# Gates stored in DRAM by groups of eight key blocks, and a ring of gated activations four deep

## The chip, the cores and the metric

The kernel runs on one core of one Trainium2 chip. The metric is the device time of one execution in microseconds, as the median over executions. The engines are named PE (TensorE), ACT (ScalarE), DVE (VectorE), POOL (GpSimd) and SP (SyncE). Everything is computed in float32 or in pairs of the reduced float32 type (a "high" and a "low" part).

## What is computed

One layer of a hybrid decoder, for 512 prompt tokens and 8 x 4 sample tokens that share the weights (D_MODEL 1024):

- h <- LN1(ALPHA h + W_out [dilated attention ; SSD scan]), with one combined input projection.
- h <- LN2(ALPHA h + PEER(h)), the part that matters here.

PEER is a retrieval of single-neuron experts. There are 128 x 128 = 16,384 experts. Each of 8 heads scores two halves of a query against 128 sub-keys, and of the sums the 16 best experts are taken, with softmax gates. So each token has 128 experts:

```
act = gelu(einsum('nd,nhkd->nhk', t, u_tab[e]))
out = einsum('nhk,nhkd->nd', g * act, v_tab[e])
```

## The kernel before

**Two ways through the experts.** The first three tiles of 128 prompt tokens (DT = 3, DEN = 384 tokens) are computed densely. For each of the PK = 128 key blocks (128 experts each) the kernel multiplies all 384 tokens with all experts of the block, applies gelu, multiplies with a dense gate table (zero where the expert wasn't chosen), and multiplies with the block's rows of peer_v. The fourth prompt tile and the sample tokens go the sparse way: POOL gathers their rows by an indirect transfer (4 KB a token, 512 KB a gather), first of peer_rows, then of peer_v, into a ring of RING = 8 buffers, and DVE takes dot products (L2022) and weighted sums (L2027) of them. Gathers go through queue q0, the direct transfers of SP through queue q1.

**The up stage** (`sp_up`, `act_up`, `pe_up`, `dve_onehots`). SP fetches a row of peer_u (L1863, 512 KB) into one of four raw buffers; ACT casts the high part (L1571), POOL or, for the later rows, DVE makes the low part (L1578, L2048); PE makes 24 matmuls of a row (`half_up`), three for each of 8 chunks (`product`, L188 to L190); ACT applies gelu into a ring (L1926), and SP stores the result to the DRAM table `act` (L1868, 192 KB). `act` lies by groups of GRP = 4 key blocks, and a group is read back in 6 KB a partition.

**The gate table** is made beside rows 68 to 115 of the up stage. There are SLABS = 12 slabs of SLAB = 32 tokens. DVE makes one-hot tables, PE multiplies them (L2014), ACT copies the result to `slab[n % 2]` (128 partitions x 128 key blocks x 32 tokens, 16 KB a partition, L1962). When a slab is complete, SP stores it (`keep_slab`, L1886) and goes on with the fetches of peer_u rows and the stores of `act`, all in q1. `keep_slab(n - 1)` stands at the start of slab n; that of the last slab stands ahead of the rows from TAIL = 116 on. SP is in order: at row 119 it waits for the last slab store and issues the first gate load, and then fetches rows 124 to 127. DVE is in order too: in the last rows it makes a low part and takes two dot products for each row.

**The value stage** (`sp_values`, `act_values`, `pe_values`, `dve_values`). For key block a, with group a // 4:

- SP loads a group's `act` (L2095, 768 KB) into one of two buffers, when DVE has finished the group before the last; the group's gates (L2099, 768 KB) right behind it, into one of two; and then four rows of peer_v (L2090, 512 KB each) into four raw buffers, each when its buffer is free.
- ACT casts the high part of the row (L2131) into a ring of eight, when PE has finished block a-8, and then the high part of the gated activations (L2135) into a ring of eight, when DVE has made the product.
- DVE multiplies activations with gates (L2208), makes the low part of the row (L2212), takes one or two late rows of the sparse way, and makes the low part of the gated activations (L2216).
- PE makes 18 matmuls (3 token tiles x 2 halves x 3 products), each 512 columns wide, all accumulated in six banks over the 128 blocks.

The semaphores start ahead (`vp_done` at 8, `ga_lo` at 2, `v_lo` at 4, `weighted` at 8), so a wait for `vp_done` of a + 1 asks for block a-8. The final layer norms follow, the first two of them inside the last blocks.

**Where the gates lie.** The DRAM table `gate` is (12 slabs, 128 partitions, 128 key blocks, 32 tokens). A slab store writes 16 KB in one run a partition. The load of a group reads, for each partition, 12 runs (one a slab) of 4 key blocks x 32 tokens, 512 B. On-chip memory is laid out by hand: `cut(at, ...)` and `overlay(at, ...)` place a buffer at `at` KB of each partition. The two rings of gated activations lie at 50 and 62, 12 KB each, the two gate buffers at 26 and 32, 6 KB each.

Of the kernel before, what the change touches and what calls it, by code (L numbers as in the profile page):

```python
# [148 lines left out]
def layer(nc, t):  # L149

    ctx = ExitStack()
    with ctx:
# [25 lines left out]
        def cut(at, *dims):  # L178
            n = int(np.prod(dims))
            assert at * KW + n <= 206 * KW, (at, dims)  # L180
            return shaped(arena[:, int(at * KW):int(at * KW) + n], dims)
# [1673 lines left out]
        def sp_up(sp):  # L1855
# [28 lines left out]
            def keep_slab(n):  # L1884
                sp.wait_ge(g_kept, n * GS + (GS + 4))
                sp.dma_start(t["gate"][n], slab[n % 2]).then_inc(slab_stored[n % 2], 16)  # L1886

# [182 lines left out]

        ga = overlay(50, 8, DEN, kind=F32R), overlay(62, 8, DEN, kind=F32R)
        agrp = [cut(at, GRP, DEN) for at in (132, 142)]
        ggrp = [cut(at, GRP * DEN) for at in (26, 32)]
        vraw, vs = overlay(10, 4, D), (overlay(152, 8, D, kind=F32R), overlay(75, 8, D, kind=F32R))
# [21 lines left out]

        def sp_gates(sp, x, par):
            g = x * 2 + par
            sp.dma_start(ggrp[par].rearrange("p (s a n) -> p s (a n)", a=GRP, n=SLAB),  # L2099
                         t["gate"].rearrange("s p a n -> p s (a n)")[:, :, bass.ds(g * (GRP * SLAB), GRP * SLAB)])\  # L2100
                .then_inc(gate_in[par], 16)

        def sp_values(sp):
            for s in range(2):
                sp.wait_ge(slab_stored[s], 16 * (1 + SLABS // 2))
            for s in range(4):
                sp.wait_ge(a_stored[s], 16 * (GROUPS + 1))
            sp.wait_ge(u_done, PK)

            def group(x, par):  # L2110
                sp_gelus(sp, x, par)
                sp_gates(sp, x, par)
                for k in range(GRP):
                    sp_rows(sp, x, par, k)

            group(0, 1)
            with sp.Fori(1, PAIRS) as x:
                for par in range(2):
                    group(x, par)
            sp.wait_ge(copied, 16 * 48)  # L2120

        def act_values(act):
# [3 lines left out]
            def pair(x, last=False):  # L2126
                for j in range(8):
# [4 lines left out]
                    if last and j == 6:  # L2132
                        act_root(act, TILES, LAST[0])
                    act.wait_ge(weighted, x * 8 + (j + 9))
                    act.copy(ga[0][:, j], prod[j % 2]).then_inc(ga_hi, 1)  # L2135

# [10 lines left out]
        def pe_values(pe):  # L2147
# [4 lines left out]
            def pair(x, first=False, last=False):  # L2152
                for j in range(8):
                    pe.wait_ge(ga_lo, x * 8 + (j + 3))
                    pe.wait_ge(v_lo, x * 8 + (j + 5))
                    for i in range(DT):
                        for half in range(2):
                            mm = product(pe, bank[:, 2 * i + half, :], [w[:, j, i * P:(i + 1) * P] for w in ga],
                                         [v[:, j, half * 512:(half + 1) * 512] for v in vs], first and j == 0, last and j == 7)
# [9 lines left out]
        def dve_values(dve):  # L2169
# [31 lines left out]
            for a in range(PK):  # L2201
                par, k, j = a // GRP % 2, a % GRP, a % 8
                rows_here = range(min(a, ROWS_END) * LATE_ROWS // ROWS_END, min(a + 1, ROWS_END) * LATE_ROWS // ROWS_END)
                if k == 0:
                    dve.wait_ge(a_in[par], 16 * (a // 8 + 1))
                    dve.wait_ge(gate_in[par], 16 * (a // 8 + 1))
                dve.wait_ge(ga_lo, a + 1)
                dve.tensor_tensor(prod[j % 2].rearrange("p (s n) -> p s n", n=SLAB),  # L2208
                                  agrp[par][:, k].rearrange("p (s n) -> p s n", n=SLAB),
                                  ggrp[par].rearrange("p (s a n) -> p s a n", a=GRP, n=SLAB)[:, :, k], ALU.mult).then_inc(weighted, 1)  # L2210
                dve.wait_ge(v_hi, a + 1)
# [3 lines left out]
                dve.wait_ge(ga_hi, a + 1)  # L2215
                dve.tensor_tensor(ga[1][:, j], prod[j % 2], ga[0][:, j].bitcast(F32), ALU.subtract).then_inc(ga_lo, 1)  # L2216
                for r in rows_here[1:]:
# [188 lines left out]
```

## Time and profile before

| | us |
|---|---|
| median of 3 runs | 2153.55 |
| lowest, highest | 2152.06, 2166.17 |
| profiled execution, its own time | 2161.72 |
| its span in the profile | 2159.3 |
| PE busy in the span | 2044.9 (95%) |
| DVE busy | 1485.2 (69%) |
| transfers, mean rate | 316 GB/s |

The profile page shows one execution. Its span begins with the first instruction and ends with the last; the rest of its own time lies around it. The up stage ends at 1592.9 us of the span, the value stage's matmuls run from 1604.8 to about 2136, and the last layer norms end the span. In the rows below, "L188" is a line of the kernel, "overlay" and "arena" are buffers in on-chip memory, "bank" is the matmul accumulator. "Share of 16 engines" is the time of the transfer records over 16 times the stretch; where records overlap it goes over 100%. "Under 2 KB" counts the records smaller than that.

### The profile page before, as it was taken

The numbers are of one execution on the slowest core, as the hardware profiler recorded it, in microseconds if no ns is written. First come the engines' busy times: TensorE is split into PE (matmuls) and PEld (weight loads), VectorE is DVE, ScalarE is ACT, GpSimd is POOL, SyncE is SP. The second block draws the span as 40 slices with busy tenths as digits, with TensorE's granted clock in tenths as the row PEclk, the third lists the DMA queues.
The fourth block names the chain that finished last, engine by engine and source line by source line (L and its number), as shares of the span: only waits on it lengthen the run. The fifth ranks groups of instructions, "written<-read, shape, count | busy, mean of one in ns | idle before, by whom it ended". The sixth has DMA issues, their size and how long they took to land.

```text
span 2159.3 us, 33707 instructions
## 1 busy us (share of the span) xinstructions
PE 2044.9 (95%) x12186; PEld 1709.8 (79%) x12186; DVE 1485.2 (69%) x3108; ACT 742.2 (34%) x1111; POOL 787.3 (36%) x485
## 2 busy tenths in 40 slices
PE   7999999998978997999999999999979999999996
PEld 7999985555542346989999999999978888778784
DVE  1375125664662333678888879999789888988888
ACT  2232113443440001224333355555433333333332
POOL 4343210000210003336898841221365564656440
PEclk9999998999988998999999999999999999999998
DMA  9999987883968668936999977888999999999992
GB/s 325 346 315 311 318 324 292 341 354 139 339 235 318 235 221 323 347 116 223 352 361 357 340 284 274 306 299 302 359 388 390 389 393 393 389 385 391 387 387 104
DMA packets 202346, 682.97 MB, mean 316 GB/s; under 512 B 18305, under 2 KB 84225, under 8 KB 194177
## 3 DMA queue, kind: packets, MB, share of 16 engines
q1 hardware_dynamic: 150832, 439.29, 56.4%
q0 software_dynamic: 46080, 167.79, 20.3%
q10 hardware_dynamic: 5328, 74.52, 9.9%
q8 instruction: 62, 1.02, 0.2%
q14 instruction: 44, 0.35, 0.0%
HBM read 618.78 MB, written 196.32 MB: 377 GB/s over the span
## 4 chain that ended last, share of the span: by engine, by line
PE 58%; DMA 19%; DVE 9%; issue 9%; POOL 3%; ACT 2%; SPq 0%; POOLq 0%; DVEq 0%; ACTq 0%
DMA overlay<-peer_v 15%; PE bank L188 12%; PE bank L189 12%; PE bank L190 12%; PE bank L1426 5%; PE bank L2014 4%; POOL overlay L358 3%; DVE overlay L2212 3%; DVE arena L2027 2%; PE bank L644 2%; PE bank L628 2%; DMA arena<-cache_v 1%; ACT overlay L2131 1%; PE bank L694 1%; PE bank L667 1%
## 5 line engine op out<-in xcount | busy, mean ns | idle before, releaser
L188 PE MATMUL bank<-overlay 128*128 128x384 f32 (+4 forms) x2832 | 959.7, 339 | 46.5 <-DVE overlay L2216 17.0
L189 PE MATMUL bank<-overlay 128*128 128x384 f32 (+4 forms) x2832 | 946.2, 334 | 0.0
L190 PE MATMUL bank<-overlay 128*128 128x384 f32 (+4 forms) x2832 | 945.2, 334 | 0.0
L188 PEld LDWEIGHTS bank<-overlay 128*128 128x128 f32 (+1 forms) x2832 | 535.4, 189 | 87.0 <-issue 39.1
L189 PEld LDWEIGHTS bank<-overlay 128*128 128x128 f32 (+1 forms) x2832 | 535.3, 189 | 30.3
L190 PEld LDWEIGHTS bank<-overlay 128*128 128x128 f32 (+1 forms) x2832 | 534.5, 189 | 31.2
L1850 POOL DMA_INDIRECT arena<-peer_v,arena x160 | 267.4, 1671 | 228.0 <-DVE arena L2027 205.1
L1578 POOL TENSOR_TENSOR overlay<-overlay 128x1024 fp32r<-128x1024 f32 x86 | 206.5, 2404 | 316.0 <-ACT overlay L1571 312.9
L2027 DVE SCALAR_TENSOR_TENSOR arena<-arena 128x1024 f32<-128x1024 f32 x160 | 204.3, 1277 | 0.1
L1850 POOL DMA_INDIRECT arena<-peer_rows,arena x80 | 106.6, 1332 | 245.8 <-DVE arena L2022 225.0
L1571 ACT CAST overlay<-overlay 128x1024 fp32r<-128x1024 f32 x144 | 150.0, 1044 | 114.7 <-DMA overlay<-peer_u 90.6
L2212 DVE TENSOR_TENSOR overlay<-overlay 128x1024 fp32r<-128x1024 f32 x128 | 155.8, 1217 | 45.2 <-ACT overlay L2131 45.2
L2131 ACT CAST overlay<-overlay 128x1024 fp32r<-128x1024 f32 x128 | 134.5, 1051 | 136.6 <-DMA overlay<-peer_v 133.8
L358 POOL TENSOR_TENSOR overlay<-overlay 128x1024 fp32r<-128x1024 f32 x44 | 105.9, 2418 | 178.6 <-ACT overlay L320 178.6
L1926 ACT ACTIVATE arena<-bank 128x384 f32<-128x384 f32 x128 | 63.7, 498 | 209.6 <-PE bank L190 204.1
L2135 ACT CAST overlay<-overlay 128x384 fp32r<-128x384 f32 x128 | 65.7, 513 | 197.6 <-DVE overlay L2208 197.6
L1426 PE MATMUL bank<-arena 128*128 128x512 f32 x256 | 120.1, 622 | 0.0
L1711 DVE SCALAR_TENSOR_TENSOR arena<-arena,bank 128x1024 f32<-128x1024 f32 x80 | 96.4, 1214 | 27.9 <-DMA arena<-peer_rows,arena 27.7
L1962 ACT COPY arena<-bank 128x512 f32<-128x512 f32 x96 | 103.6, 1131 | 33.1 <-PE bank L2014 33.0
L2058 DVE TENSOR_SCALAR arena<-arena 128x128 f32<-128x128 f32 x384 | 106.4, 349 | 0.0
L1426 PEld LDWEIGHTS bank<-arena 128*128 128x128 f32 x256 | 49.0, 198 | 66.1 <-issue 64.6
L2014 PE MATMUL bank<-arena 128*128 128x128 f32 x768 | 101.0, 274 | 0.0
(235 smaller groups left out, 2160.9 us busy)
## 6 DMA issues: line engine op xcount, KB each, us to landing
overlay<-peer_u SPq DMA_DIRECT2D x128, 512.0 KB, 7.6
overlay<-peer_v SPq DMA_DIRECT2D x128, 512.0 KB, 11.3
o_ks<-cache_k ACTq DMA_DIRECT2D x11, 4088.0 KB, 18.4
o_vsall<-cache_vall SPq DMA_DIRECT2D x21, 2044.0 KB, 23.5
arena<-cache_kT SPq DMA_DIRECT2D x32, 896.0 KB, 11.2
arena<-cache_v SPq DMA_DIRECT2D x56, 512.0 KB, 6.9
arena<-w_out SPq DMA_DIRECT2D x48, 512.0 KB, 5.6
act<-arena SPq DMA_DIRECT2D x128, 192.0 KB, 8.2
```

Of the source, the lines that this page charges most:

```text
L188: pe.matmul(out, lhs[0], rhs[0], start=start, stop=False)
L189: pe.matmul(out, lhs[0], rhs[1], start=False, stop=False)
L190: return pe.matmul(out, lhs[1], rhs[0], start=False, stop=stop)
L358: pool.tensor_tensor(ws[1][:, s], wraw[:, s], ws[0][:, s].bitcast(F32), ALU.subtract).then_inc(w_lo, 1)
L1426: mm = pe.matmul(bank[:, 2 * (i % 2) + half, :], mixT[:, c, i * P:(i + 1) * P], w[:, half * 512:(half + 1) * 512], start=(c == 0), stop=(c ...
L1571: act.copy(us[0][:, s], uraw[s]).then_inc(u_hi, 1)
L1578: pool.tensor_tensor(us[1][:, s], uraw[s], us[0][:, s].bitcast(F32), ALU.subtract).then_inc(u_lo, 1)
L1850: pool.indirect_dma_start(gring[g % RING], None, table, bass.IndirectOffsetOnAxis(ap=at, axis=0)).then_inc(row_in[g % RING], 16)
L2014: mm = pe.matmul(bank[:, 4 + w % 4, j * P:(j + 1) * P], hot_b[:, w % 2, j], hot_a[:, w % 2, j], start=True, stop=True)
L2027: dve.scalar_tensor_tensor(acc, gring[r], w[:, bass.ds(j, 1)], acc, ALU.mult, ALU.add).then_inc(row_done, 1)
L2131: act.copy(vs[0][:, j], vraw[:, k]).then_inc(v_hi, 1)
L2212: dve.tensor_tensor(vs[1][:, j], vraw[:, k], vs[0][:, j].bitcast(F32), ALU.subtract).then_inc(v_lo, 1)
```

## The change

The gate table becomes (16 pairs of groups, 128 partitions, 12 slabs, 8 x 32). A slab store writes, for each partition, 16 runs of 1 KB, one for each pair. A gate load now covers a pair of groups (eight key blocks) and reads 12 KB in one run a partition, 1.5 MB in all; there are 16 of them in place of 32. The gate buffers are 12 KB each. To make room the rings of gated activations hold four blocks in place of eight: their high parts lie at 50, the low parts at 56, and the second gate buffer at 62, where the low parts lay. ACT's copy into the ring gets a wait of its own for PE to have finished block a-4. The load of the next pair is issued with the second group of a pair, between that group's `act` and its peer_v rows; DVE waits for gates once a pair. SP's loop is written over two pairs at a time, so that the buffer is known when the program is built.

```diff
             def keep_slab(n):
                 sp.wait_ge(g_kept, n * GS + (GS + 4))
-                sp.dma_start(t["gate"][n], slab[n % 2]).then_inc(slab_stored[n % 2], 16)
+                sp.dma_start(t["gate"][:, :, n].rearrange("x p m -> p x m"), slab[n % 2].rearrange("p (x a) n -> p x (a n)", a=8)).then_inc(slab_stored[n % 2], 16)
...
-        ga = overlay(50, 8, DEN, kind=F32R), overlay(62, 8, DEN, kind=F32R)
+        ga = overlay(50, 4, DEN, kind=F32R), overlay(56, 4, DEN, kind=F32R)
...
-        ggrp = [cut(at, GRP * DEN) for at in (26, 32)]
+        ggrp = [cut(at, 8 * DEN) for at in (26, 62)]
...
-        def sp_gates(sp, x, par):
-            g = x * 2 + par
-            sp.dma_start(ggrp[par].rearrange("p (s a n) -> p s (a n)", a=GRP, n=SLAB),
-                         t["gate"].rearrange("s p a n -> p s (a n)")[:, :, bass.ds(g * (GRP * SLAB), GRP * SLAB)])\
-                .then_inc(gate_in[par], 16)
+        def sp_gates(sp, x, odd):
+            sp.dma_start(ggrp[odd], t["gate"][bass.ds(x, 1)].rearrange("x p s n -> p (x s n)")).then_inc(gate_in[odd], 16)
...
-            def group(x, par):
+            def group(x, par, odd, more=True):
                 sp_gelus(sp, x, par)
-                sp_gates(sp, x, par)
+                if par == 1 and more:
+                    sp_gates(sp, x + 1, 1 - odd)
                 for k in range(GRP):
                     sp_rows(sp, x, par, k)
 
-            group(0, 1)
-            with sp.Fori(1, PAIRS) as x:
-                for par in range(2):
-                    group(x, par)
+            group(0, 1, 0)
+            with sp.Fori(0, PAIRS // 2 - 1) as y:
+                for odd in (1, 0):
+                    for par in range(2):
+                        group(y * 2 + (2 - odd), par, odd)
+            for par in range(2):
+                group(PAIRS - 1, par, 1, False)
...
+                    act.wait_ge(vp_done, x * 8 + (j + 5))
                     act.wait_ge(weighted, x * 8 + (j + 9))
-                    act.copy(ga[0][:, j], prod[j % 2]).then_inc(ga_hi, 1)
+                    act.copy(ga[0][:, j % 4], prod[j % 2]).then_inc(ga_hi, 1)
...
                 if k == 0:
                     dve.wait_ge(a_in[par], 16 * (a // 8 + 1))
-                    dve.wait_ge(gate_in[par], 16 * (a // 8 + 1))
+                if j == 0:
+                    dve.wait_ge(gate_in[a // 8 % 2], 16 * (a // 16 + 1))
...
-                dve.tensor_tensor(ga[1][:, j], prod[j % 2], ga[0][:, j].bitcast(F32), ALU.subtract).then_inc(ga_lo, 1)
+                dve.tensor_tensor(ga[1][:, j % 4], prod[j % 2], ga[0][:, j % 4].bitcast(F32), ALU.subtract).then_inc(ga_lo, 1)
...
-    t["gate"] = nc.dram_tensor("gate", (DEN // SLAB, P, PK, SLAB), F32, kind="Internal").ap()
+    t["gate"] = nc.dram_tensor("gate", (PK // 8, P, DEN // SLAB, 8 * SLAB), F32, kind="Internal").ap()
```

PE's matmuls index the ring with `j % 4`, and the product on DVE reads the gates of block a at `[:, j]` of its pair's buffer in place of `[:, k]` of its group's.

## Rows read from the trace of the kernel before

**Rows 1.** The page: busy tenths, transfer share and rate in 40 slices.

```profile
PE   7999999998978997999999999999979999999996
DMA  9999987883968668936999977888999999999992
GB/s 325 346 315 311 318 324 292 341 354 139 339 235 318 235 221 323 347 116 223 352 361 357 340 284 274 306 299 302 359 388 390 389 393 393 389 385 391 387 387 104
```

**Rows 2.** Stretches: us, busy PE, PEld, DVE, ACT, POOL (x count), clock, share, GB/s.

```profile
1640.00:1830.00 190.00, 190.00 (x839) 157.24 (x839) 168.78 (x199) 67.12 (x90) 100.36 (x62) 1.00 1.05 391
1830.00:2105.00 275.00, 269.40 (x1176) 219.33 (x1175) 241.56 (x284) 98.77 (x131) 149.52 (x85) 1.00 1.04 389
```

**Rows 3.** Waits from 1640 us on: us in total, times, longest.

```profile
ACT overlay L2131 <- DMA overlay<-peer_v: 131.5, 57, 6.6
...
PE bank L188 <- DVE overlay L2216: 5.0, 5, 1.5
```

**Rows 4.** Transfers, 1650 to 2100 us: records, MB, share of 16 engines.

```profile
DMA packets 82244, 175.25 MB, mean 389 GB/s; under 512 B 4913, under 2 KB 46385, under 8 KB 82236
...
q1 hardware_dynamic: 61276, 98.85, 61.0%
q0 software_dynamic: 20960, 76.33, 43.4%
```

**Rows 5.** PE timeline at 2037.8 us: start, length, instruction, idle before.

```profile
2037.77 0.49 PE L188 MATMUL bank<-overlay 128*128 128x512 f32 x1 [1.52 <-DVE overlay L2216]
```

**Rows 6.** Transfers from 1562.6 to 1564.0 us (gate load).

```profile
DMA packets 830, 0.50 MB, mean 357 GB/s; under 512 B 10, under 2 KB 816, under 8 KB 830
...
q1 hardware_dynamic: 830, 0.50, 112.4%
```

**Rows 7.** Transfers from 1546 to 1550 us (slab store).

```profile
DMA packets 162, 1.70 MB, mean 424 GB/s; under 512 B 4, under 2 KB 4, under 8 KB 77
...
q1 hardware_dynamic: 89, 1.41, 84.3%
q0 software_dynamic: 73, 0.29, 17.5%
```

**Rows 8.** Transfers from 1990.3 to 1992.3 us.

```profile
q0 software_dynamic: 172, 0.65, 85.6%
q1 hardware_dynamic: 170, 0.11, 18.9%
```

**Rows 9.** Timeline of ACT and of PE for block 15 of the value stage.

```profile
1658.92 0.52 ACT L2135 CAST overlay<-overlay 128x384 fp32r<-128x384 f32 x1 [3.00 <-DVE overlay L2208]
...
1667.47 0.39 PE L188 MATMUL bank<-overlay 128*128 128x512 f32 x1
```

**Rows 10.** Transfers by kind: count, KB each, median us to landing.

```profile
act<-arena SPq DMA_DIRECT2D x128, 192.0 KB, 8.2
gate<-arena SPq DMA_DIRECT2D x12, 2048.0 KB, 8.1
```

**Rows 11.** Timeline of DVE and of PE for peer_u row 112.

```profile
1506.91 1.23 DVE L2048 TENSOR_TENSOR overlay<-overlay 128x1024 fp32r<-128x1024 f32 x1 [1.72 <-ACT overlay L1571]
...
1517.01 0.42 PE L188 MATMUL bank<-overlay 128*128 128x384 f32 x1
```

**Rows 12.** Timeline of SyncE's transfers at the last slab store.

```profile
1542.89 0.34 SPq L1886 DMA_DIRECT2D gate<-arena  x1
1543.29 0.42 SPq L1863 DMA_DIRECT2D overlay<-peer_u  x1
```

**Rows 13.** Timeline of ACT and of PE at peer_u row 120.

```profile
1556.50 1.05 ACT L1571 CAST overlay<-overlay 128x1024 fp32r<-128x1024 f32 x1 [10.50 <-DMA overlay<-peer_u]
...
1558.86 0.45 PE L188 MATMUL bank<-overlay 128*128 128x384 f32 x1 [0.74 <-DVE overlay L2048]
```

**Rows 14.** Queue 0, 1543.5 to 1555 us, then 1543.5 to 1560 us.

```profile
q0 software_dynamic: 464, 1.71, 36.6%
...
q0 software_dynamic: 715, 2.61, 38.8%
```

More of the change, by code:

```diff
@@ L2157, in pair @@
                         for half in range(2):
-                            mm = product(pe, bank[:, 2 * i + half, :], [w[:, j, i * P:(i + 1) * P] for w in ga],
+                            mm = product(pe, bank[:, 2 * i + half, :], [w[:, j % 4, i * P:(i + 1) * P] for w in ga],
                                          [v[:, j, half * 512:(half + 1) * 512] for v in vs], first and j == 0, last and j == 7)
@@ L2209, in dve_values @@
                                   agrp[par][:, k].rearrange("p (s n) -> p s n", n=SLAB),
-                                  ggrp[par].rearrange("p (s a n) -> p s a n", a=GRP, n=SLAB)[:, :, k], ALU.mult).then_inc(weighted, 1)
+                                  ggrp[a // 8 % 2].rearrange("p (s a n) -> p s a n", a=8, n=SLAB)[:, :, j], ALU.mult).then_inc(weighted, 1)
                 dve.wait_ge(v_hi, a + 1)
```

## Prediction

> **What bounds the kernel now.** I read the slices of the page first, then one table of stretches over the value stage, then who waits for whom there, and then the transfers of single stretches. The slices [rows 1] show two things at their limit at once over the last fourteen slices: PE at nine tenths and the transfer engines at nine tenths, at 385 to 393 GB/s.
>
> The stretches [rows 2] say which of them ends the work. From 1640 to 1830 us PE issues 839 matmuls in 190.0 us, 0.2265 us each, without a gap. A key block has 18 of them (DT 3, two halves, three products), so 4.08 us, and a pair of groups (8 blocks) 32.6 us. From 1830 to 2105 PE is busy 269.4 of 275 us. The waits [rows 3] say the same: PE stood 5.0 us in five stops, all for the low part of a gated activation (L2216), while ACT waited 131.5 us for peer_v. So PE is the bound and the transfers are only just behind it: 27 groups passed in the 450 us of [rows 4], 33.3 us a pair against PE's 32.6. PE starts the stage ahead and uses up its lead; the first stop is at 1835.8, one later one is in [rows 5]. The most that faster gate transfers can return in this stage is these 5.0 us. This is the first choice I make: a stage whose transfer engines are full all the time has only 5 us to give.
>
> **The gate loads.** A load of a group is 1536 runs of 512 B. In a stretch that holds little else [rows 6], 830 records took 112.4% of 16 x 1.4 us, that is 25.2 us, so 30.3 ns each. The 27 loads of [rows 4] are 41,472 records, 1257 us or 17.5% of the 7200 us that 16 engines have in 450 us. They carry 21.2 MB. All the rest, 154 MB, took 104.7 - 17.5 = 87.2%, which is 24.5 bytes a ns. At this rate the same 21.2 MB in 12 KB runs take 865 us, 12.0%. The need falls by 5.5 of 104.7 parts, so a pair from 33.3 to about 31.5 us, below PE's 32.6. Then the lead is no longer used up, and the five stops go: -5.0 us. (I take the whole, since 1.1 us a pair over 14 pairs is more than the 5.0.)
>
> Row against rule: the stretch of 512 B runs moves 357 GB/s [rows 6], that of 16 KB runs 424 [rows 7]. The Trainium skill (DMA: Bandwidth & Descriptors, Specifications) puts line rate at 512 B and more. By that rule the old gate loads cost nothing extra and this term is 0 (the first rival); by the rows it is -5.0, and the measurement decides.
>
> There is a second effect of run size. In [rows 8], gate runs and gathered rows are both waiting: 170 records of q1 and 172 of q0 go in 2 us, one for one, though q0's are 4 KB and take 85.6% of the time. A stream of small runs gets its turns but few bytes. Gate loads in 12 KB runs turn this round, so the peer_v rows behind them in q1 come earlier. It helps, and adds nothing beyond the 5.0.
>
> **A load of 1.5 MB at once.** Ahead of the odd group's rows in q1 now stand 0.79 MB of activations and 1.57 MB of gates, before 0.79 and 0.79. With one row of 0.52 MB that is 2.9 MB, 7.4 us at 391 GB/s, 10 to 11 us with gathers taking turns (in bytes 4 KB against 6 or 12 KB). The row is wanted four blocks, 16.3 us, after its buffer came free. Even groups carry 0.79 MB less than before. I take 0; if PE's lead did run out, see the rivals. The first such load stands behind an empty lead at 1599 us: with all eight gathers outstanding it may push row 4 some 2 us back, against a lead of about 3 us there (by the timeline, block 3). 0.
>
> **The ring of gated activations, eight to four.** ACT's cast (L2135) of block a now also waits until PE has finished a-4. So it may run three blocks, 12.2 us, ahead of PE's start. In the old trace it seldom wants to: in [rows 9] the cast of block 15 starts at 1658.92 and PE starts that block at 1667.47, 8.6 us later; over all 128 blocks PE stood one or two blocks behind at 121 and three at 6, never four. After the change the lead will reach the limit, and then ACT stands with DVE's L2216 and the next product (L2208) behind it; PE has 12.2 us of work at that time and DVE needs some 4 us a block. 0. The wait for gates moves from each group to each pair, the loads are issued a pair ahead, and SP has half as many: 0, both hidden behind PE.
>
> **The slab stores.** [rows 10] has the stores of both kinds as the trace lists them. A slab of 2.1 MB goes out in 2048 runs of 1 KB instead of 128 of 16 KB. Price of the runs: none in the trace is 1 KB. Below, a 1 KB run costs what its bytes cost at 424 GB/s [rows 7], nothing added. Above, it costs two 512 B records, 60.6 ns, so the slab 2048 x 60.6 / 16 = 7.8 us instead of 4.9: +2.9 us. Between them: 512 B at 26.5 bytes a ns (424/16) are 19.3 ns, so 11.0 of the 30.3 ns are a fixed part, and 1024 B take 38.6 + 11.0 = 49.6 ns, the slab 6.35 us: +1.4. I take that; it is in the middle of the two ends. Eleven of the twelve stores are covered: in [rows 11] the low half of a row is ready at 1508.14 and PE begins it at 1517.01. This 8.9 us is the smallest lead from 1280 to 1550 us.
>
> The twelfth is not covered. It is issued at 1542.89 and the fetch of peer_u row 120 right behind it [rows 12]. ACT stands 10.5 us for this row until 1556.50, DVE makes the low half until 1558.8, and PE starts the row at 1558.86 after standing 0.74 us [rows 13]. What delays the store now delays PE one for one. With 16 KB runs the store takes 84% of the engines' time [rows 7], and the gathers wait. With 1 KB runs the turns are the same but four bytes of q0 go for one of q1: the gathers go first. How many are there: q0 moved 1.71 MB to 1555 and 2.61 MB, all five that POOL had issued, to 1560 [rows 14]. At most the 0.90 MB that now pass after row 120 pass before it: 0.90 / 0.415 = 2.2 us. The bounds of this edit are then 0 (the gathers aren't there in time, no price per run) and 2.2 + 2.9 = 5.1 us. I take 1.4 + 1.6 = 3.0 us: the price above and some three quarters of the turn effect, since POOL issues the five rows one after another and not all can pass ahead. Rows 124 to 127 are fetched after it with 1.7 us of lead, behind the first gate load, which is 0.79 MB larger (1.9 us); but the gathers that would share with it are gone by then. 0. The rest of the passage to the value stage, the 12 us in which PE waits from 1592.9 to 1604.8, hangs on the last store of activations and moves as a whole.
>
> **Sum.** -5.0 + 3.0 = -2.0 us. The profiled execution took 2161.7 us, of them 2159.3 its span: 2159.7 is what I expect of such an execution. The median of the runs is 2153.55, 8.2 below; I carry the difference over: 2151.5.
>
> **Rivals.**
> First, a 512 B run costs only what its bytes cost, and the loads took longer in [rows 6] for another reason; or the freed time doesn't reach PE, since DVE is busy 88 to 89% of the first two stretches of [rows 2]. For it: the five stops fall in a minority of the pairs, so little decides. Against it: 5.5 parts of 105. The stops stay and only the store counts: 2156.5. The line-rate rule of the Trainium skill named above (DMA: Bandwidth & Descriptors, Specifications) leads to the same time.
> Second, slower: stores in 1 KB runs to DRAM are much slower than loads in 512 B runs. Place: each of the twelve stores, with peer_u rows queued behind. It decides from the point where a store occupies q1 longer than the 5 to 7 us of now plus the 8.9 us of lead. At 100 GB/s it takes 21 us, and each store costs 21 - 15 = 6 us, the last 14: about +80, less the 5, so 2229. Against it: activations are stored in 1.5 KB runs beside everything else and land in 8.2 us [rows 10].
> Third, slower by less: the 2.4 MB burst at each odd group makes peer_v late, PE stops 1 to 2 us (the size of the stop in [rows 5]) in each of 14 pairs instead of 5.0 in all: +9 to +23, with the store's 3.0 from 2166 to 2180, say 2170. It decides once a row takes longer than four blocks from its fetch to its cast. Against it, the 16.3 us above.
>
> **Chances.** Forecast 0.80, first rival 0.12, second 0.03, third 0.05. This kernel's runs scatter by half a per cent and more, so 1% (21.5 us) is about what can be told from no change. Faster by over 1% needs PE to do less, and nothing here does that: 0.02, for what I don't see. Slower by over 1% is the second rival and the upper part of the third: 0.04. Within 1%: 0.94. Range: terms -5.0 to 0 and 0 to +5.1, with 1 us for the clock after a longer stop, give 2148.5 to 2160; the scatter of a median of runs (2152.1 to 2166.2 shown) widens the lower end: 2145 to 2160.
>
> **What would show it.** Right: under 2 KB some 41,000 records fewer in the value stage and about 380 to 390 GB/s there at a share clearly below 1.05; PE's waits on L2216 after 1640 us near 0; ACT's L2135 or L2131 waiting for PE; PE's stop before row 120 up from 0.74 to between 2 and 5 us; the slab store landing 2 to 3 us later in the last case only. Wrong: PE waits for DVE's L2048 in several slabs (second rival), or PE stops after odd groups (third), or the five stops stay.

## The result and the profile after

| | before | changed |
|---|---|---|
| median of 20 runs, us | 2157.29 | 2163.39 |
| lowest, highest | 2145.77, 2166.17 | 2151.92, 2170.30 |
| profiled execution, span | 2159.3 | 2165.9 |

The changed kernel is slower: the ratio of its runs to those of before is 1.0028, 95% interval 1.0014 to 1.0041, about 6 us. That is inside the 1% that was given 0.94, but on the other side of the forecast -2.0 us and beyond the range. The forecast median of 2151.5 stood on three runs of before (2153.55); over 20 runs its median is 2157.29, so 3.7 of the 11.9 us between forecast and result belong to that base, and 8.1 to the change (+6.1 in place of -2.0).

The slices of the changed kernel's page, to hold against [rows 1]:

```profile
PE   7999999998979997999999999999879999999996
PEclk9999998999978998999999999999989999999998
DMA  8999897884968678927999978888999999999981
GB/s 325 349 326 344 301 341 280 348 319 161 330 222 309 235 251 314 350 92 238 351 365 352 323 278 284 288 290 291 353 370 397 412 413 410 403 395 404 394 334 69
```

The value stage (the last ten slices) now moves up to 413 GB/s where it moved 393 at most, and its last two slices fall to 334 and 69: its transfers are done sooner. The 29th slice (1516 to 1570 us) has an 8 for PE where [rows 1] has a 9.

Next, stretches of the changed kernel's value stage, as in [rows 2]:

```profile
1660.00:1830.00 170.00, 170.00 (x751) 140.81 (x750) 158.54 (x186) 62.83 (x86) 87.05 (x58) 1.00 1.02 412
1830.00:2110.00 280.00, 280.00 (x1237) 231.91 (x1236) 258.43 (x301) 101.67 (x138) 84.81 (x87) 1.00 0.98 389
```

PE is busy 450.0 of 450.0 us. Who waits from 1640 us on (against [rows 3]):

```profile
ACT overlay L2137 <- PE bank L190: 267.2, 105, 2.6
...
ACT overlay L2132 <- DMA overlay<-peer_v: 11.0, 9, 3.2
```

PE's wait for the low part of the gated activations (now L2219) is gone from the list. ACT's cast into the ring (now L2137) stands 105 times for PE: the lead is at its limit of three blocks. ACT's wait for peer_v fell from 131.5 us to 11.0.

The transfers from 1650 to 2100 us (against [rows 4]):

```profile
DMA packets 43905, 181.63 MB, mean 404 GB/s; under 512 B 4880, under 2 KB 4880, under 8 KB 42142
...
q1 hardware_dynamic: 22156, 102.38, 56.7%
q0 software_dynamic: 21740, 79.16, 44.4%
```

The 41,500 small records are gone, and more bytes move in less engine time, 101.1% for 104.4%. So the value stage did what was forecast, and more. The loss is ahead of it. Waits of the changed kernel from 1275 to 1560 us, where the gate table is made:

```profile
ACT overlay L1571 <- DMA overlay<-peer_u: 89.2, 15, 8.7
DVE overlay L2048 <- ACT overlay L1571: 29.0, 11, 3.9
...
PEld bank L2014 <- DVE arena L2058: 8.7, 9, 1.5
PE bank L2014 <- DVE arena L2058: 6.0, 7, 1.2
```

PE waits for L2058, the one-hot tables on DVE. In the same rows of before (1277 to 1550 us) this wait isn't in the list at all, and ACT's wait for peer_u is 65.6 us there.

Because the code ahead of the gate table is the same in all kernels but its duration isn't (last section), I compare stages from PE's first matmul of peer_u row 72. "Gap" is PE's idle time between its last matmul of the up stage and the first of the value stage, and "norms" is what follows the value stage's last matmul. The table is worked out from PE's timeline, of one profiled execution each; these are the changed kernel's lines for its bounds, the first matmul of rows 72, 119 and 120, the last of row 127 and the first of the value stage:

```profile
1275.71 0.42 PE L188 MATMUL bank<-overlay 128*128 128x384 f32 x1
...
1560.69 0.34 PE L188 MATMUL bank<-overlay 128*128 128x384 f32 x1
...
1569.84 0.69 PE L188 MATMUL bank<-overlay 128*128 128x384 f32 x1 [4.77 <-DVE overlay L2048]
...
1606.18 0.34 PE L190 MATMUL bank<-overlay 128*128 128x384 f32 x1
...
1619.36 0.76 PE L188 MATMUL bank<-overlay 128*128 128x512 f32 x1 [12.84 <-DVE overlay L2219]
```

| kernel | rows 72 to 119 | 119 to 120 | 120 to end of up | gap | value stage | norms | from row 72 on |
|---|---|---|---|---|---|---|---|
| before | 276.7 | 5.1 | 34.0 | 12.0 | 534.9 | 19.6 | 882.3 |
| changed | 285.0 | 9.2 | 36.7 | 12.8 | 526.6 | 19.9 | 890.2 |
| e1, stores only | 286.3 | 8.7 | 36.2 | 12.9 | 535.2 | 19.6 | 898.8 |
| e2, loads only | 276.7 | 5.2 | 35.9 | 11.7 | 535.1 | 19.9 | 884.5 |
| e3, changed, store later | 276.7 | 4.2 | 40.0 | 12.4 | 526.6 | 19.9 | 879.8 |
| e4, before, store later | 276.7 | 4.2 | 40.2 | 12.4 | 534.4 | 19.5 | 887.5 |
| f1, ACT's queue | 276.7 | 4.2 | 45.8 | 10.5 | 526.3 | 19.6 | 883.1 |
| f2, gathers held | 284.4 | 4.2 | 34.2 | 12.8 | 526.9 | 19.9 | 882.3 |
| f3, stores of 4 KB | 277.3 | 7.4 | 34.0 | 12.2 | 534.6 | 19.6 | 885.0 |
| f4, ring alone | 276.7 | 4.2 | 33.9 | 10.9 | 535.7 | 19.6 | 881.1 |
| g1, order and hold | 276.7 | 4.2 | 34.3 | 12.8 | 527.2 | 19.9 | 875.1 |
| g2, ACT's queue and hold | 276.7 | 4.2 | 41.8 | 12.5 | 527.1 | 19.5 | 881.8 |
| g3, loads halved | 276.7 | 4.3 | 36.8 | 11.8 | 526.5 | 19.5 | 875.6 |
| g4, first load split | 276.7 | 4.6 | 40.3 | 11.9 | 526.4 | 19.5 | 879.5 |

A full row of PE is 4.2 us. The changed kernel loses 8.3 us in rows 72 to 119, 4.0 at row 120, 2.7 behind it and 0.9 in the gap, and gains 8.3 in the value stage: +7.9 in all.

### The profile page after: what moved, and what is told of

Same layout as the page of the kernel before. It is cut to its first block, busy times and chain, and to the rows that moved or that the text cites. A ratio compares the mean times of both kernels' runs of the same rounds, so it can differ in the third digit from the quotient of the medians.

```text
span 2165.9 us, 33621 instructions
## 1 busy us (share of the span) xinstructions
PE 2050.4 (95%) x12186; PEld 1715.4 (79%) x12186; DVE 1490.7 (69%) x3108; ACT 737.5 (34%) x1111; POOL 710.6 (33%) x485
## 4 chain that ended last, share of the span: by engine, by line
PE 80%; DMA 9%; DVE 8%; issue 2%; ACT 1%; SPq 0%; POOL 0%; DVEq 0%; ACTq 0%; POOLq 0%
PE bank L188 20%; PE bank L189 20%; PE bank L190 20%; DMA overlay<-peer_u 6%; PE bank L1426 5%; PE bank L644 2%; PE bank L628 2%; DVE arena L2058 2%; DVE overlay L2048 1%; PE bank L694 1%; PE bank L2014 1%; PE bank L667 1%; DVE arena L2022 1%; DVE arena L2054 1%; DMA arena<-cache_v 1%
## 5 line engine op out<-in xcount | busy, mean ns | idle before, releaser
L188 PE MATMUL bank<-overlay 128*128 128x384 f32 (+4 forms) x2832 | 959.3, 339 | 43.9 <-DVE overlay L2219 12.8
L189 PEld LDWEIGHTS bank<-overlay 128*128 128x128 f32 (+1 forms) x2832 | 534.9, 189 | 30.8
L1850 POOL DMA_INDIRECT arena<-peer_v,arena x160 | 193.0, 1206 | 290.6 <-DVE arena L2027 264.7
L2137 ACT CAST overlay<-overlay 128x384 fp32r<-128x384 f32 x128 | 65.7, 514 | 311.7 <-PE bank L190 267.2
L2132 ACT CAST overlay<-overlay 128x1024 fp32r<-128x1024 f32 x128 | 134.3, 1049 | 11.1 <-DMA overlay<-peer_v 11.0
L2058 DVE TENSOR_SCALAR arena<-arena 128x128 f32<-128x128 f32 x384 | 107.2, 359 | 0.0
L2014 PEld LDWEIGHTS bank<-arena 128*128 128x128 f32 x768 | 98.5, 191 | 8.7 <-DVE arena L2058 8.7
```

Source lines behind the costliest of these rows:

```text
L188: pe.matmul(out, lhs[0], rhs[0], start=start, stop=False)
L189: pe.matmul(out, lhs[0], rhs[1], start=False, stop=False)
L1850: pool.indirect_dma_start(gring[g % RING], None, table, bass.IndirectOffsetOnAxis(ap=at, axis=0)).then_inc(row_in[g % RING], 16)
L2014: mm = pe.matmul(bank[:, 4 + w % 4, j * P:(j + 1) * P], hot_b[:, w % 2, j], hot_a[:, w % 2, j], start=True, stop=True)
L2058: mm = dve.tensor_scalar(hot_b[:, w % 2, j], const("iota"), at(1), at(2), ALU.is_equal, ALU.mult)
L2132: act.copy(vs[0][:, j], vraw[:, k]).then_inc(v_hi, 1)
```

## The experiments

**The change in two halves.** The first run has the new table and stores, with everything else of before:

```diff
-                sp.dma_start(t["gate"][n], slab[n % 2]).then_inc(slab_stored[n % 2], 16)
+                sp.dma_start(t["gate"][:, :, n].rearrange("x p m -> p x m"), slab[n % 2].rearrange("p (x a) n -> p x (a n)", a=8)).then_inc(slab_stored[n % 2], 16)
...
+            sp.dma_start(ggrp[par].rearrange("p (s m) -> p s m", m=GRP * SLAB),
+                         t["gate"][bass.ds(x, 1)].rearrange("x p s m -> p (x s) m")[:, :, par * GRP * SLAB:(par + 1) * GRP * SLAB])\
```

> The kernel before with the new DRAM table and its slab stores in 1 KB runs; each group's gates are still loaded by themselves in 512 B runs, and the ring of gated activations is eight deep. Theory (the loss lies in the 1 KB stores, which hold up SP's queue in front of the peer_u fetches; the gain lies in the loads): the twelve stores are issued over some 272 us in place of 264, PE waits for L2058 about 6 us in all, the stop before row 120 is 4 to 5 us, and the value stage keeps its five stops. 13 to 15 us slower than before, ratio 1.006 to 1.007. Rival (the loss comes with the larger gate load or the ring of four): within 2 us of before, stores over 264 us.

Ratio 1.0079 (1.0057 to 1.0100), 16.5 us more than before from row 72 on, a little above the expected 13 to 15. The waits of this kernel, first from 1275 to 1560, then from 1640 us on:

```profile
PEld bank L2014 <- DVE arena L2058: 9.8, 8, 2.0
PE bank L2014 <- DVE arena L2058: 7.2, 8, 1.7
...
PE bank L188 <- DVE overlay L2216: 4.8, 5, 1.9
```

The whole loss comes with the stores, and without the new loads the five stops are back. The rival (ring or large load) falls.

The second run is the changed kernel with the old table and stores:

```diff
-            sp.dma_start(ggrp[odd], t["gate"][bass.ds(x, 1)].rearrange("x p s n -> p (x s n)")).then_inc(gate_in[odd], 16)
+            sp.dma_start(ggrp[odd].rearrange("p (s m) -> p s m", m=8 * SLAB),
+                         t["gate"].rearrange("s p a n -> p s (a n)")[:, :, bass.ds(x * (8 * SLAB), 8 * SLAB)]).then_inc(gate_in[odd], 16)
```

> The changed kernel with the old DRAM table and its stores in 16 KB runs; a pair's gates are read in twelve runs of 1 KB a partition, the ring is four deep, the gates are loaded a pair ahead. Theory: stores over 264 us, no waits for L2058, stop before row 120 under 1.5 us, the stops for the low part of the gated activations gone from the value stage or nearly (1 KB runs give back two thirds of what 12 KB runs do). 5 to 8 us faster than before, ratio 0.996 to 0.998. Rival (ring or large load to blame): slower than before, with PE stops in the value stage.

The rows before the value stage are as expected. The value stage is not: 535.1 us, with these waits from 1640 us on:

```profile
ACT overlay L2133 <- DMA overlay<-peer_v: 101.0, 35, 8.6
...
PE bank L188 <- DVE overlay L2220: 5.3, 6, 2.2
```

And its transfers from 1650 to 2100 us:

```profile
DMA packets 60642, 175.14 MB, mean 389 GB/s; under 512 B 4699, under 2 KB 24667, under 8 KB 60634
...
q1 hardware_dynamic: 39767, 99.08, 58.3%
q0 software_dynamic: 20867, 75.98, 43.0%
```

The engines' time fell from 104.4 to 101.3%, and nothing was gained in this stage. So engine time, the term on which I based the forecast, doesn't decide alone. The timed runs have it at 1.0047 (1.0022 to 1.0073), more than the 2.2 us of its profile; this difference stays open.

**The place of the store in SP's queue.** The same move in the changed kernel and in that of before:

```diff
             for n in range(SLABS):
-                if n:
-                    keep_slab(n - 1)
                 for k in range(UPS):
                     next_row(EARLY + n * UPS + k)
+                    if n and k == 1:
+                        keep_slab(n - 1)
...
-            keep_slab(SLABS - 1)
             for a in range(TAIL, PK):
                 next_row(a)
+                if a == TAIL + 2:
+                    keep_slab(SLABS - 1)
```

> The changed kernel; each slab store is issued behind the peer_u fetches of the first two rows of the next slab in place of ahead of them, the last one behind those of rows 120 to 122. Theory (SP is in order: it stands for the finished slab while raw buffers are free, so the fetch behind it is late, and a longer store makes it later): no waits of PE for L2058, stores over 264 us or less, stop before row 120 gone, and the value stage as short as in the changed kernel: 14 to 18 us faster than it, 8 to 11 us faster than before, ratio 0.995 to 0.996. Rival (the 1 KB runs take time and turns from all that runs beside them, wherever they stand): stores still over 268 us or more and PE waits for L2058 remain, at most 5 us faster than the changed kernel.

> The kernel before with the same move of the slab stores behind the fetches. Theory: no PE wait to save in the slabs, only the stop of 0.74 us before row 120: 0 to 3 us faster than before, value stage with its five stops. Rival (the order also sets when gathers and rows arrive later on): more than 4 us either way.

Both have rows 72 to 119 in 276.7 us, and no stop before row 120: the loss in the slabs is the place in the queue, since the runs of 1 KB are the same. Instead both take 40 us behind row 120, where before takes 34.0 and the changed kernel 36.7: ratios 0.9992 (0.9966 to 1.0019) and 1.0021 (1.0007 to 1.0034). SP's timeline of the first of them, with lines left out, shows how:

```profile
1532.10 0.39 SPq L1886 DMA_DIRECT2D gate<-arena  x1
1532.54 15.95 SPq L1863 DMA_DIRECT2D overlay<-peer_u  x1
...
1557.35 0.34 SPq L2099 DMA_DIRECT2D arena<-gate  x1
1557.74 1.55 SPq L1863 DMA_DIRECT2D overlay<-peer_u  x1
```

The last store is issued at 1532.10 and lands 25.2 us later. The next issue takes 15.95 us, the first gate load waits for the store until 1557.35, and the fetch of row 124 stands behind it. PE then stops 1.0 us at row 123 and 3.05 us at row 124; most of what is left of the 6 us goes at a lower granted clock (0.71 over row 124). In the second kernel, with 16 KB runs, the last store lands after 16.3 us and PE stops 3.3 us at row 124: the late place costs about as much with either run size. My expectation had only the gain; the rival for the second of them, more than 4 us either way, came true.

**The store on another queue.**

```diff
+                act.wait_ge(g_kept, n * GS + (GS + 4))
+                act.dma_start(t["gate"][:, :, n].rearrange("x p m -> p x m"), slab[n % 2].rearrange("p (x a) n -> p x (a n)", a=8)).then_inc(slab_stored[n % 2], 16)
...
-                if a == TAIL + 3:
+                if a == TAIL + 5:
```

> The changed kernel; ACT issues each slab store (1 KB runs) on its own queue right after its last copy of the slab, so that SP neither stands for the slab nor for the store's descriptors; the first gate load two rows later. Theory (in the changed kernel the store stands in SP's queue ahead of the fetches, and SP's next transfer is held while the store's many descriptors wait): rows 72 to 119 in 276.7 us as before, no stop before row 120 (4.21 us from row 119 to 120), 34 to 35 us from there to the end of the up stage, value stage 526.6 us; 872 to 875 us from row 72 to the end against 882.3 before and 890.2 changed, ratio to before 0.995 to 0.997. Rival (the runs take the time from the fetches wherever they are issued): rows 72 to 119 over 280 us, or a stop of 2 us and more before row 120.

276.7 us and no stop at row 120: the first two parts of the theory hold. SP's issue behind each store takes 0.33 us here. The stores land later than in the changed kernel, and in the slabs this costs PE nothing, so there it is not the store's own length that counts but what stands behind it. Their landings are now

```profile
DMA to landing us min/median/max: 12.3/13.5/37.7
```

and the last one, 37.7 us, holds SP's first gate load and the fetches behind it, here SP's and PE's lines:

```profile
1560.89 0.33 SPq L1863 DMA_DIRECT2D overlay<-peer_u  x1
...
1586.08 0.33 SPq L2093 DMA_DIRECT2D arena<-gate  x1
1586.45 0.43 SPq L1863 DMA_DIRECT2D overlay<-peer_u  x1
...
1598.56 0.69 PE L188 MATMUL bank<-overlay 128*128 128x384 f32 x1 [9.69 <-DVE overlay L2043]
```

A stop of 9.7 us, at row 126. Ratio 1.0018 (0.9995 to 1.0041).

**The gathers' turns.** The changed kernel, with POOL held from gather 55 until the last store has landed:

```diff
+                if g == HOLD:
+                    pool.wait_ge(slab_stored[1], 16 * (1 + SLABS // 2))
```

> The changed kernel; POOL holds the gathers from number 55 on until the last slab store has landed. Nothing is left out. Theory (a queue of 1 KB runs takes turns one for one with the gathers' 4 KB runs): the last store lands in 9 to 11 us in place of 16.4, SP's next transfers are issued in under 4 us in place of 4.0 and 6.1, and PE's stop before row 120 falls from 4.8 to 1 to 2 us. Rival (the price is in the runs themselves): store still over 14 us, stop 4 us and more.

```profile
1547.09 0.39 SPq L1889 DMA_DIRECT2D gate<-arena  x1
1547.54 3.09 SPq L1866 DMA_DIRECT2D overlay<-peer_u  x1
...
1557.57 0.74 SPq L2101 DMA_DIRECT2D arena<-gate  x1
```

The last store lands 8.6 us after its issue; in the changed kernel it was 16.4 us. The first gate load, which stands behind it and four fetches, is issued 10.5 us after it. PE has no stop before row 120 at all, less than the 1 to 2 us expected, and there is no low clock behind it: 34.2 us for 36.7. From row 119 to the end of the up stage it takes back 7.4 us. The slabs keep their loss (284.4 us), but this says nothing of the gathers' part in it: the hold begins at about 1541 us, between the eleventh and the twelfth store, and up to there each slab has its four gathers as before. One execution was timed (2158.37 us), so the profile is what counts here.

The gathers do have a part in the slabs. From the issue of a slab store to the landing of the peer_u row behind it, the mean over the first eleven stores is 9.7 us and 0.37 MB of gathers in the kernel before, 11.9 us and 0.91 MB in the changed one (worked out from SP's issues and the records of q0). No run held the gathers in the slabs, so how the 2.2 us divide between the price of the runs and the turns stays open.

**Run size of the store alone.** The table by 32 key blocks, stores in 4 KB runs, loads in 512 B runs:

```diff
+                sp.dma_start(t["gate"][:, :, n].rearrange("q p m -> p q m"), slab[n % 2].rearrange("p (q a) n -> p q (a n)", a=32)).then_inc(slab_stored[n % 2], 16)
```

> The kernel before with the table by groups of 32 key blocks: slab stores in 4 KB runs, group loads in 512 B runs, ring of eight; SP's loop over the groups is written out. Theory (run size against the gathers' 4 KB and the count of descriptors decide): stores land in 7.5 to 8.2 us in the slabs, rows 72 to 119 in 276.7 us without waits for L2058, stop before row 120 1 to 3 us, value stage 534 to 536 us with its stops. Rival (any spread of the store over strided runs hurts): rows 72 to 119 over 280 us as with 1 KB.

Rows 72 to 119 take 277.3 us, and the stop before row 120 about 3 us: between 16 KB and 1 KB in both, as the run size would have it. The rival falls. The slabs lose 0.6 us, where no loss was expected. One execution was timed, 2165.86 us. The landings, minimum, median and maximum, go 7.4/8.1/11.1 us with 16 KB, 7.6/8.7/13.3 with 4 KB, 8.5/9.3/16.4 with 1 KB.

**The ring alone**, in the kernel of before:

```diff
-        ga = overlay(50, 8, DEN, kind=F32R), overlay(62, 8, DEN, kind=F32R)
+        ga = overlay(50, 4, DEN, kind=F32R), overlay(56, 4, DEN, kind=F32R)
...
+                    act.wait_ge(vp_done, x * 8 + (j + 5))
```

> The kernel before with the ring of gated activations four deep and ACT's added wait, nothing else. Theory (the ring costs nothing while PE is seldom more than two blocks behind): value stage 534 to 536 us, stops 5 to 6 us in all. Rival (the ring of four halves what PE's early lead can cover): the first stop comes before 1750 us of the span and the value stage takes 538 us or more.

The value stage takes 535.7 us (534.9 before), with stops of 4.7 us; ACT waited for PE at the casts 1.7 us in all. The ring costs nothing that one profile can tell. The one timed execution took 2176.25 us; its PE reached row 72 only at 1293.0 us (1277.0 in before), ahead of all that the edit touches, so the stages are what can be compared.

**The two remedies together.** First: the stores behind two fetches in the slabs, the last one in its old place, the gathers held:

> The changed kernel; in the slabs each store is issued behind the fetches of the next slab's first two rows, the last store stays ahead of row 120's fetch as in the changed kernel, and POOL holds the gathers from number 55 on until it has landed. Theory (both losses are the store's place in SP's queue and its turns against the gathers, each taken away): rows 72 to 119 in 276.7 us, 4.2 us to row 120, 34 to 35 us to the end of the up stage, value stage 526 to 527 us; 873 to 875 us from row 72 to the end, against 882.3 before, ratio to before 0.995 to 0.997. Rival (the transfers saved in one place are asked for in another, as in the last two attempts): a new stop of 3 us or more in the rows from 120 on, ratio 0.999 or more.

Every stage as expected, 875.1 us from row 72 on. The last store lands after 8.4 us. Median 2151.01 beside 2158.67, ratio 0.9960 (0.9941 to 0.9980): faster than before, and so than the changed kernel. Second: ACT's queue with the gathers held:

> The changed kernel with the stores on ACT's own queue, the gathers held from number 55 on until the last one has landed, and the first gate load two rows later. Theory (the last store took 37.7 us on its own queue because the gathers and SP's rows each take a turn for each of its 1 KB runs): it lands in 10 to 20 us, the stop of 9.7 us at row 126 goes, 871 to 875 us from row 72 to the end, ratio 0.995 to 0.997. Rival (SP's rows alone are enough to starve it): landing over 25 us and a stop of 3 us or more.

The last store lands in 18.6 us instead of 37.7, but PE stops all the same, 5.8 us at 1560.7, and the up stage ends 7.5 us later than in the first. Ratio 0.9996 (0.9972 to 1.0019). Here the hold is the trouble, since the store that ends it lands so much later (8.4 us in the first). POOL's and DVE's timelines:

```profile
1550.64 0.94 POOL L1853 DMA_INDIRECT arena<-peer_rows,arena  x1 [28.49 <-DMA gate<-arena]
...
1558.18 1.23 DVE L2020 SCALAR_TENSOR_TENSOR arena<-arena 128x1024 f32<-128x1024 f32 x1 [16.27 <-DMA arena<-peer_rows,arena]
```

Without the stall of DVE behind a late peer_u row, DVE comes to gather 55 sooner; POOL has held it for 28.5 us (18.2 in the first) and DVE stands 16.3 us for it, with the low half of the next row behind. Neither rival nor theory had this.

**Turns in the value stage.** The loads-only kernel with each pair's load in two halves of six slabs, one with each group:

```diff
                 if par == 1 and more:
-                    sp_gates(sp, x + 1, 1 - odd)
+                    sp_gates(sp, x + 1, 1 - odd, 0)
+                if par == 0:
+                    sp_gates(sp, x, odd, 1)
```

> The kernel of the loads-only run (old table, gates read in 1 KB runs, ring of four), each pair's load in two halves of six slabs, one with each group. Theory A (what makes peer_v late is the number of runs in a row that each wait for a turn of the gathers): value stage 527 to 531 us, stops under 2.5 us in all. Theory B (the mean rate decides: 1 KB runs free too little): value stage 534 to 536 us with 4 to 6 us of stops, as with whole loads.

The value stage takes 526.5 us (one execution was timed, 2161.12 us). Its waits from 1640 us on have no line of PE for DVE at all, and its transfers from 1650 to 2100 us are

```profile
DMA packets 62594, 179.29 MB, mean 398 GB/s; under 512 B 5038, under 2 KB 25785, under 8 KB 62586
...
q1 hardware_dynamic: 41122, 101.08, 58.9%
q0 software_dynamic: 21464, 78.14, 43.9%
```

The runs are the same 1 KB as in the loads-only run, and so are their number and price; only 768 stand in a row in front of peer_v instead of 1536. Theory A holds: the whole 8.6 us are there. The bytes in a row don't decide, since the changed kernel reads the same 1.5 MB at once, in 128 runs of 12 KB, without a stop. What fits all four kernels is how many runs in a row a peer_v row has to wait behind, each of which may wait for a gather's 4 KB: 1536 (before and loads-only) give 534.9 and 535.1 us, 768 and 128 give 526.5 and 526.6. The new table wasn't needed for this gain: this kernel has the old one, with its 16 KB stores, and is at 875.6 us from row 72 on, beside 875.1 for the changed kernel with both remedies.

The last run puts the second half of the very first load three rows later (`if a == TAIL + 6: sp_gates(sp, 0, 0, 1)`):

> The kernel of the halved loads (old table, slab stores in 16 KB runs ahead of the fetches, gates in 1 KB runs in halves of six slabs, ring of four), with the second half of the very first load three rows later. Theory (runs in a row behind the gathers' turns are what delays a row in q1): no stop of PE in the rows from 121 to 127, 34 us from row 120 to the end of the up stage, value stage 526 to 527 us, 871 to 874 us from row 72 to the end against 882.3 before, ratio to before 0.995 to 0.997. Rival (the gain of the halved loads in one profile was chance): value stage 530 us and more with stops, ratio 0.999 or more.

The value stage repeats (526.4 us, no stops), which makes chance unlikely for the gain. But the stop of 2.5 us that the halved loads had at row 124 didn't go; there is one of 3.4 us at row 127 instead, and 40.3 us from row 120 on where 34 were expected. Ratio 0.9982 (0.9964 to 1.0001). In these runs whatever is put between the last fetches delays the one behind it.

## Why the prediction was wrong, point by point

**The gate loads: right in mechanism, too small, and with the wrong reason for its size.** The five stops went, as forecast. I took their idle time, 5.0 us; the stage became 8.3 us shorter. PE's starts in the trace of before show the rest: 5.8 us from start to start at the five stops, and six smaller losses of 0.23 to 0.27 us each (some just behind a stop) that the wait list doesn't have, 1.5 us; the remainder is of smaller ones still. The other part is the reason. I said that the turns (one record of q1 for one of q0) help and add nothing beyond the freed engine time. It is rather that they decide: with 1 KB runs in one burst a part of the engine time was freed and none of the gain came; with the same runs in two bursts all of it came. The first rival, by which the stops would have stayed, fell. The line-rate rule of the Trainium skill (DMA: Bandwidth & Descriptors, Specifications) would have had no gain at all from 512 B on; the value stage's 8.3 us stand against it as far as this kernel, with gathers beside the loads, can say.

**The ring, the larger load, the later wait for gates: 0, right.** Ring alone +0.8 us. In the changed kernel ACT waited 267.2 us for PE, as foreseen, and PE never for it.

**The slab stores in the slabs: the step that failed.** I wrote "Eleven of the twelve stores are covered" and took as cover the 8.9 us by which the low half of a row leads PE [rows 11]. That lead hardly changed: in the changed kernel it is 8.5 us or more in every row from 72 to 115. It was the wrong cover. DVE is in order, and the instruction behind the low half (L2048) is the next one-hot table (L2054, L2058), which PE wants within a few us. The changed kernel behind the store issued at 1375.97, first SP, then ACT, DVE and PE's weight loads:

```profile
1375.97 0.38 SPq L1886 DMA_DIRECT2D gate<-arena  x1
1376.40 3.03 SPq L1863 DMA_DIRECT2D overlay<-peer_u  x1
...
1387.37 1.05 ACT L1571 CAST overlay<-overlay 128x1024 fp32r<-128x1024 f32 x1 [7.39 <-DMA overlay<-peer_u]
...
1388.44 1.23 DVE L2048 TENSOR_TENSOR overlay<-overlay 128x1024 fp32r<-128x1024 f32 x1 [1.94 <-ACT overlay L1571]
1389.59 0.69 DVE L2054 TENSOR_TENSOR arena<-arena 128x512 f32<-128x512 f32 x1
1390.19 1.11 DVE L2058 TENSOR_SCALAR arena<-arena 128x128 f32<-128x128 f32 x4
...
1391.35 0.97 PEld L2014 LDWEIGHTS bank<-arena 128*128 128x128 f32 x8 [0.23 <-DVE arena L2058]
```

The same slab of before:

```profile
1383.97 1.04 ACT L1571 CAST overlay<-overlay 128x1024 fp32r<-128x1024 f32 x1 [5.08 <-DMA overlay<-peer_u]
...
1385.05 1.23 DVE L2048 TENSOR_TENSOR overlay<-overlay 128x1024 fp32r<-128x1024 f32 x1 [1.04 <-ACT overlay L1571]
```

Here DVE caught up before PE felt it. The store itself is longer by about what I had said (median landing 9.3 us for 8.1, +1.2 against +1.4). The row behind it is later by more, 2.2 us on the mean, and SP's next issue takes 3.03 us where it took 0.43. The cover can be read from the timelines of before, from the end of a one-hot table on DVE to PE's first weight load of it. Over the 96 tables it is 0.2 to 3.0 us. For the first table behind the late row of each slab (its sixth) it is 0.23 to 2.49, 1.53 on the mean of the eleven; in the changed kernel it is down to 0.05 us in nine of the eleven, and there PE waits. So 1.5 us could be covered; 2.2 - 1.5 = 0.7 us are left a slab, and the slabs cost 8.3 us, 0.75 for each of eleven. I had priced the store's own length rightly, left the gathers' turns out of the slabs, and above all asked the wrong instruction how much was covered.

**The twelfth store: right in mechanism, too small.** Forecast +3.0, bounds 0 to 5.1. The stop grew from 0.74 to 4.77 us (+4.0), between the two. Holding the gathers took all of it away, but that takes away more than the change had added. From the store's issue to the landing of row 120's fetch (17.6 us in place of 13.6), q0 moved 2.62 MB in place of 2.09: by bytes the turns cost 0.53 / 0.415 = 1.3 us, not more than the 1.6 that I gave them. In the same time q1 moved 0.7 MB more (4.27 for 3.56), and the mean rate was 392 GB/s for 416; neither was in my sum. Outside the term were 2.7 us of low clock, for which I had 1 us in the range only: after the stop the granted clock is 0.58 on the mean over row 120, near the lower of PE's two levels (1.2 of 2.4 GHz), where before there was no such stretch. Rows 119 and 120 in the changed kernel, columns as in [rows 2]:

```profile
1560.70:1564.90 4.20, 4.20 (x25) 4.05 (x24) 0.00 (x0) 0.00 (x0) 0.00 (x0) 1.00 1.03 411
1569.80:1577.00 7.20, 7.16 (x25) 7.16 (x26) 7.20 (x11) 3.40 (x5) 5.19 (x3) 0.58 1.02 423
```

**The sum**: forecast -5.0 + 3.0; found -8.3 + 8.3 + 7.6 + 0.3 for the rest, +7.9 from row 72 on. The second rival had the place right (peer_u rows queued behind each store) and its point of decision wrong: not 8.9 us, but 1.5 us of lateness on the mean. A slip in the prediction changes nothing: the shares of [rows 4] add up to 104.4, not 104.7.

## What to carry to other kernels

The cover of a delayed transfer is the shortest lead among all that stands behind it on each in-order engine it passes, not the lead of its own consumer: follow the wait through ACT and DVE to what is queued behind it. Where two queues share the transfer engines, count records and not bytes: a long row of small runs in one queue passes the engines on to the other, and what stands behind in the first pays; so put fetches that are wanted first ahead of such a row, cut the row into parts, or hold the other queue for that time. A better layout for the reader that costs the writer small runs paid here only with the writer's place in the queue moved and the gathers held beside the last store (0.9960). The two remedies without the new layout weren't run; by the table they could save no more than the 0.9 us that before loses at row 120. Halving the loads of the old layout gave the value stage the same time.

## What the runs showed of the hardware

- Queues that had work at the same time moved about equally many records, whatever their size: 170 of q1 (512 B) and 172 of q0 (4 KB) in [rows 8]; and while the last store was in flight on ACT's queue (1549 to 1586 us), 2064 of ACT's queue (1 KB), 1727 of SP's (1.5 and 4 KB) and 2229 of the gathers' (4 KB). What this can do shows at the end of the up stage: the same last store of 2 MB in 1 KB runs landed in 8.4 and 8.6 us with the gathers held, in 16.4 with them, in 25.2 behind more fetches and in 37.7 on ACT's queue. In 16 KB runs it took 11.1 us, and 16.3 behind more fetches.
- The issue of a transfer took long on SP when a transfer of many small runs was ahead of it in the same queue. Behind a store of 2048 runs it was 1.3 to 4.0 us in the changed kernel, 2.7 us and more in eleven of twelve, and behind the last one the second issue took 6.1 us more; once, with the store behind more fetches, it was 15.95 us. Behind a store of 128 runs it was 0.4 us in ten of twelve, 1.4 at most. SP issued nothing else meanwhile.
- The code ahead of row 72 is the same in all these kernels, but PE reached row 72 anywhere from 1265.4 to 1293.0 us in the profiled executions. Over the 20 timed runs of the changed kernel, time and mean granted clock go together (correlation -0.87, clock 0.966 to 0.975). Whether the clock is the cause wasn't tested. This scatter makes a single execution's time worth little here, while the stage from row 72 on repeats: 276.7 us in ten of the fourteen profiles.
